# RWKV-7 rounds: K's factor, K product, seeds and K rows moved behind steps of the state chain, and one decay product for both directions

## What is computed

```
def _rwkv7_scan(r, w, k, v, kk, a, S0):
    def step(S, inp):
        rt, wt, kt, vt, kkt, at = inp
        sa = einsum('rbhvk,rbhk->rbhv', S, -kkt)
        S = S * wt[..., None, :] + sa[..., None] * (kkt * at)[..., None, :] + vt[..., None] * kt[..., None, :]
        return S, einsum('rbhvk,rbhk->rbhv', S, rt)

k_dir = k[:, :, None, :] * (1 + (a - 1) * k_a)
```

## Time and profile before

| | |
|---|---|
| time, median of 3 runs | 2148.57 us (2144.32 to 2149.24) |
| time of the profiled execution | 2146.77 us |
| span in the trace, first to last instruction | 2145.0 us (1.8 us lie around it) |
| mean granted TensorE clock | 0.940 |
| PE busy | 1885.8 us (88%) |
| DVE, ACT, POOL busy | 1031.2, 602.7, 719.9 us (48%, 28%, 34%) |
| the rounds of branch c, about 698 to 1121 us | some 423 us |

### The profile page before, as it was taken

One profiled execution on the slowest core, in us unless ns is written; L12 is line 12 of the kernel. 1 busy time (PEld: TensorE's weight loads), 2 busy tenths in 40 slices (PEclk: granted clock), 3 DMA queues, 4 the chain that ended last, 5 costly groups with the idle time before them and its releaser, 6 DMA issues. The chain is left out here.

```text
span 2145.0 us, 49387 instructions
## 1 busy us (share of the span) xinstructions
PE 1885.8 (88%) x20834; PEld 1763.5 (82%) x20834; DVE 1031.2 (48%) x1726; ACT 602.7 (28%) x1335; POOL 719.9 (34%) x560
## 2 busy tenths in 40 slices
PE   5599799998994778888773699999999999999998
PEld 3589798877992677777662599999999999999998
DVE  6703753777227454444538745434344343434254
ACT  4413244322114545455430224101111010202034
POOL 4402331442425322222302231343434353343460
PEclk8799898998998899899995699999999999999999
DMA  9554110021110000000000300111202111111122
GB/s 305 184 179 165 31 31 22 17 89 30 40 30 10 4 7 4 4 4 4 4 21 16 118 20 20 40 49 34 60 26 56 30 48 49 29 49 34 44 60 89
DMA packets 148180, 110.31 MB, mean 51 GB/s; under 512 B 13298, under 2 KB 144393, under 8 KB 147757
## 3 DMA queue, kind: packets, MB, share of 16 engines
q1 hardware_dynamic: 148013, 107.83, 16.5%
HBM read 93.17 MB, written 14.55 MB: 50 GB/s over the span
## 5 line engine op out<-in xcount | busy, mean ns | idle before, releaser
L253 PE MATMUL banks<-Z_r 128*128 128x384 f32 x2016 | 350.8, 334 | 0.0
L253 PEld LDWEIGHTS banks<-Z_r 128*128 128x128 f32 x2016 | 349.5, 188 | 0.3
L2641 DVE SCALAR_TENSOR_TENSOR XT<-banks,MOD,XT 128x128 f32 x224 | 110.7, 515 | 226.1 <-PE banks L253 225.3
L2975 ACT ACTIVATE PAD<-banks 128x384 f32<-128x384 f32 x96 | 47.2, 492 | 503.2 <-PE banks L2870 503.0
L3091 DVE TENSOR_TENSOR PAD<-PAD 128x384 f32<-128x384 f32 x96 | 99.0, 1031 | 142.9 <-ACT PAD L2975 142.8
L235 POOL TENSOR_TENSOR Z_r<-Z,ones 128x512 fp32r<-128x512 f32 x56 | 77.1, 1376 | 254.6 <-DMA Z<-in_mlp_w 254.6
L235 POOL TENSOR_TENSOR W_r<-Z,ones 128x1024 fp32r<-128x1024 f32 x32 | 77.1, 2409 | 240.4 <-DMA Z<-in_mlp_w 240.4
L2870 PE MATMUL banks<-HT_r,W_r 128*128 128x384 f32 x768 | 149.1, 335 | 2.4 <-ACT HT_r L2942 1.6
L2870 PE MATMUL banks<-YT_r,W_r 128*128 128x384 f32 x768 | 148.6, 334 | 0.0
L2870 PE MATMUL banks<-HT_r,Z_r 128*128 128x384 f32 x768 | 148.5, 334 | 0.0
L2870 PEld LDWEIGHTS banks<-HT_r,W_r 128*128 128x128 f32 x768 | 134.5, 188 | 3.3 <-issue 1.9
(11 more groups left out here) (413 smaller groups left out, 4052.7 us busy)
## 6 DMA issues: line engine op xcount, KB each, us to landing
Z<-in_w_mod SPq DMA_DIRECT2D x16, 1024.0 KB, 5.2
Z<-in_mlp_w SPq DMA_DIRECT2D x32, 512.0 KB, 4.2
Z<-in_mlp_w SPq DMA_DIRECT2D x58, 256.0 KB, 2.7
YT<-in_w_in SPq DMA_DIRECT2D x18, 512.0 KB, 3.9
XT<-in_w_mod SPq DMA_DIRECT2D x8, 1024.0 KB, 11.0
residual<-Z SPq DMA_DIRECT2D x1, 4608.0 KB, 17.5
low_part<-XT_r SPq DMA_DIRECT2D x1, 4608.0 KB, 15.6
XT<-low_part SPq DMA_DIRECT2D x8, 576.0 KB, 5.3
```

Of the source, the lines that this page charges most:

```text
L253: mm = nc.tensor.matmul(self.bank(slot, g), w[slot][:, k, :], x(k, g), start=(n == 0 and k == 0), stop=(n == 2 and k == self.blocks - 1))
L2641: ins = nc.vector.scalar_tensor_tensor(out=x, in0=S.PS[3 * slot + g][:, a:b], scalar=S.MOD[:, ds(col, 1), c:c + 1].rearrange("p a b -> p ( ...
L2975: nc.scalar.activation(R[slot][:, grp(g)], up.bank(slot, g), ACT.Relu).then_inc(up.drained[g].sem, 1)
```

## The change

Five edits, all in the rounds:

1. ACT: `q_act` and `u_act` of j = 0 stand ahead of `ka_act`.
2. DVE: the product of the state with the decay is one instruction over both directions (128x384) where it was two (128x192). For that, POOL stores the backward direction's two chunk-end decays in reversed order, so that column j is right for both directions.
3. POOL: the ones onto the diagonals come first. Then POOL waits for `new_state` of j = 0 (in rounds with a chain), makes the K product, and then the seeds.
4. DVE: the K rows come behind `zm_dve` of step 0, before `state_dve` of j = 1.
5. POOL waits for its own K product ahead of the seeds (an order that the list has anyway).

```diff
--- before.py
+++ after.py
@@ -2210,13 +2210,14 @@
 
     def round_act(act, chain, nxt, after, par):
         r, n, a = chain, nxt, after
+        if r is not None:
+            q_act(act, r, 0)
+            u_act(act, r, 0)
         if n is not None:
             tok = direction_tiles(act, n)[0]
             for d in range(2):
                 ka_act(act, n, d, tok[d])
         if r is not None:
-            q_act(act, r, 0)
-            u_act(act, r, 0)
             q_act(act, r, 1)
             u_act(act, r, 1)
         for d in range(2):
@@ -2283,10 +2284,9 @@
         heads = lambda x: x.rearrange("p d q n -> p (d q) n")
         nc.vector.tensor_tensor(heads(C.S), heads(C.S), by_block(bank(6)), ALU.add).then_inc(f["added"].sem, 1)
         done(dve, "added", r, j + 1)
-        for d in range(2):
-            ins = nc.vector.tensor_tensor(C.S[:, d, :, :], C.S[:, d, :, :],
-                                          C.ends[par][:, d, :, chunk(d, j)].unsqueeze(2).to_broadcast([P, NP, N]), ALU.mult)
-        ins.then_inc(f["new_state"].sem, 1)
+        ends = C.ends[par].rearrange("p d q j -> p (d q) j")[:, :, j]
+        nc.vector.tensor_tensor(heads(C.S), heads(C.S), ends.unsqueeze(2).to_broadcast([P, 2 * NP, N]),
+                                ALU.mult).then_inc(f["new_state"].sem, 1)
         if between:
             between()
         if j:
@@ -2332,8 +2332,6 @@
                 done(dve, "gram_l", n, d + 1)
                 nc.vector.tensor_tensor(C.LP[:, d, :, :, :].rearrange("p c q n -> p (c q) n"), by_block(bank(d)),
                                         mask(d, LEVELS, 2 * NP), ALU.mult).then_inc(f["masked_l"].sem, 1)
-            for d in range(2):
-                k_rows_dve(dve, n, d)
         if r is not None:
             state_dve(dve, r, par, 0, tiles, first if n is not None else None)
         elif n is not None:
@@ -2341,6 +2339,8 @@
         if n is not None:
             zm_dve(dve, n, 0, 0)
             zm_dve(dve, n, 0, 1)
+            for d in range(2):
+                k_rows_dve(dve, n, d)
         if r is not None:
             state_dve(dve, r, par, 1, tiles)
         if n is not None:
@@ -2378,7 +2378,8 @@
     def r_rows_pool(pool, a, d, par, tok):
         end = N if d == 0 else 0
         done(pool, "exped", a, d + 1)
-        nc.gpsimd.tensor_copy(C.ends[par][:, d, :, :], C.EP[:, d, :, :, end]).then_inc(f["ends"].sem, 1)
+        ends = C.EP[:, d, :, :, end]
+        nc.gpsimd.tensor_copy(C.ends[par][:, d, :, :], ends[:, :, ::-1] if d else ends).then_inc(f["ends"].sem, 1)
         for p in range(NP):
             ins = nc.gpsimd.tensor_tensor(tile_cols(C.RR[par][:, d, :, :], p),
                                           S.Z[:, p, ds(tok, P)].rearrange("p (c n) -> p c n", n=N),
@@ -2388,9 +2389,6 @@
     def round_pool(pool, chain, nxt, after, par):
         r, n, a = chain, nxt, after
         if n is not None:
-            tok = direction_tiles(pool, n)[0]
-            for d in range(2):
-                k_dir_pool(pool, n, d, tok[d])
             for d in range(2):
                 done(pool, "masked_l", n, d + 1)
                 nc.gpsimd.tensor_tensor(C.LP[:, d, :, :, :].rearrange("p c q n -> p (c q) n"),
@@ -2399,6 +2397,12 @@
                                             f["unit_l"].sem, 1)
             before(pool, "tz", n)
             done(pool, "unit_l", n, 2)
+            if r is not None:
+                done(pool, "new_state", r, 1)
+            tok = direction_tiles(pool, n)[0]
+            for d in range(2):
+                k_dir_pool(pool, n, d, tok[d])
+            done(pool, "k_dir", n, 2)
             for d in range(2):
                 for h in range(2):
                     x = rows_of(h)
```

## The result

| | before | after |
|---|---|---|
| median (4 runs of each, side by side) | 2146.45 us (2142.76 to 2149.24) | **2122.3 us** (2118.47 to 2127.98) |
| time of the profiled execution | 2146.77 us | 2118.47 us |
| span in the trace | 2145.0 us | 2115.5 us |
| rounds, first mask of the prologue to the last sum into Y | 411.5 us | 385.55 us |
| PE's wait for the copy of Q (list) | 12.3 us | 5.7 us |

The ratio is 0.9891, with an interval of 0.9862 to 0.9919: 23 us faster, between 17 and 30.

A forecast was written before the change was run, and what follows sets the result against it. It took the bound to be a chain passing between engines, mostly PE, with PE's idle time winnable. 6.4 + 9.1 - 2.5 - 1.0 plus 0.5 for the clock made 12.5 us: forecast 2135.0 us, range 2125 to 2144.

The forecast's parts named there:

- Part 1: ACT's factor behind the copies: PE's wait for Q falls from 1.50 to 0.58 us in seven rounds, gaining 6.4 us.
- Part 2: One state product on DVE with POOL still: PE's wait ahead of j = 1 becomes 1.33 us, gaining 9.1 us.
- Part 3: POOL's K products and seeds behind `new_state`: PE newly waits for seeds, 0.3 us over eight rounds, costing 2.5 us.
- Rival A: Each K row holds POOL's seeds up 0.56 us; eight rounds lose 0.9 us each; total gain 7 us; chance 0.17.
- Part 4: DVE's K rows behind `zm_dve`: they end at about +6 us from PE's restart, delay `tanh_act`, and cost nothing.
- The prologue: Before the chain, K products ahead of the seeds delay `tz_pe` of d = 1: costs 1 us, bounds 0 and 2.5.
- Clean rounds: Rounds at full clock take 41.3 to 41.6 us, from 43.3; over 42.3 us would mean the prediction is wrong.
- The clock: Falls to half speed behind PE's waits become fewer but are drawn anew by the spacing: 0.5 us gained.
- rival D: With shorter PE waits, clock falls become rare: 8 us more gained, 2127 us; chance 0.13.
- The stock of what could be won: Time lost to low clock in rounds 2 to 5, against the clean 43.3 us: over 10 us.
- The prediction's own test: Prediction is wrong if time lost to low clock differs from 10 us by more than 8.
- The base: Gains subtracted from the profiled execution's 2146.8 us, which stood 1.8 us under the median of 2148.6.

The follow-up runs named there:

- q_first: Kernel before with only ACT's copies of Q and U of j = 0 moved ahead of K's factor: 2145.34 us, ratio 1.0025.
- all_but_q: Changed kernel with K's factor back ahead of ACT's copies of Q and U: 2133.92 us, ratio 0.9966 to the kernel before.
- one_product: Kernel before with only the state product merged into one instruction, POOL's seeds still beside it: 2134.69 us, ratio 0.997.
- two_products: Changed kernel with the state product split into two instructions again, POOL still idle beside them: 2124.62 us, ratio 0.9935 to the kernel before.
- before_warm24: Kernel before with 24 useless matmuls in PE's wait for the state product: 2138.25 us, ratio 0.9978.
- both_warm: Kernel before with useless matmuls in both PE waits, 24 in the state product's and 12 in Q's: 2136.73 us, ratio 0.998.
- seeds_early: Changed kernel with three of POOL's four seeds ahead of its wait for `new_state`, K products last: 2122.92 us, ratio 0.9917 to the kernel before.
- before_warm: Kernel before with 48 useless matmuls in PE's wait for the state product: 2144.63 us, ratio 1.0018.
- after_hole: Changed kernel with an unused 0.96 us DVE reduction between sum and state product of j = 0: 2133.37 us, ratio 0.9957 to the kernel before.

## Why the prediction was right or wrong

**Waits against times, all kernels.** The sum of waits is what the lists show against the kernel before's 12.3 + 21.1 us; the prologue's 0.5 us is left out; the measured difference is the ratio's, at 2142 us.

| kernel | by the waits | measured (interval) | time at the lower clock, change (estimate) |
|---|---|---|---|
| q_first | +6.2 | +5.4 (+1.5 to +9.2) | +2 |
| all_but_q | -5.9 | -7.3 (-11.3 to -3.2) | -16 |
| one_product | -5.1 | -6.4 (-10.3 to -2.6) | -12 |
| two_products | -11.6 | -13.9 (-20 to -8) | -22 |
| changed kernel | -12.4 | -23 (-30 to -17), again -20 (-27 to -13) | again -34 |
| before_warm24 | 0 | -4.7 (-7.7 to -1.7) | -22 |
| both_warm | 0 | -4.3 (-7.1 to -1.3) | -29 |

The last column is an estimate of mine from all runs: every run has the mean granted clock of its whole execution on record, and twice the missing share times the span is its time at 1.2 GHz. The column is the kernel's mean less that of the kernel before beside it, in us, each good to about 10 (to 15 or so where there are only 6 or 7 runs). The 93 executions of the kernel before have a mean clock of 0.941, 253 us at the lower level; the 11 of the changed kernel have 0.948, 220 us. That is 32 us less (23 to 42). Among the 93, each us more at the lower level went with 0.28 us more of time (0.22 to 0.33), which is what the rounds gave above. So the clock's share in the lasting gain is some **9 us** (6 to 12), provided that the time at the lower level is what made those executions longer.

**Part 1: held.** 0.57 us in every round, list 12.3 to 5.7 us: 6.6 won, 6.4 forecast. But the step was costed as if it stood alone, and alone it loses 5 us (q_first). The prediction gave as cover "some 5 us ahead of the next thing that ACT owes PE"; it left out that DVE's K rows, through POOL, wait for the factor too, ahead of the state's sum. In the full change edit 4 had moved them, so no number was wrong; the parts are not to be added one by one.

**Part 2: held.** 18 products of 557 ns, none longer than 560, 0.56 forecast:

```profile
L2288 DVE TENSOR_TENSOR PAD<-PAD,misc x18: 557/557/560, 746.9 to 1090.0; 128x384 f32<-128x384 f32 x18
```

The wait is 1.34 us (1.33 forecast), the list 12.1 (12.0 forecast). Of its two causes, POOL's standing still would have done nearly all of it alone (two_products), which the prediction did not say.

**Part 3: held.** 0.29 us in a clean round where 0.3 was taken, 1.4 us in the one round that has no decay products of tile a between PE's restart and `tz_pe`; 3.2 us in the list over seven waits and 0.89 more in the prologue, where 2.5 and 1.0 were counted. Rival A, the seeds that bind, did not come. (Its own sum was loose: from +6.1 to +7.1 is 1.0 us a round and 8 us in eight, where it has 0.9 and 7.5.) With two K rows beside them the four seeds took 4.28 us, where 3.86 had been with the two products of the state and three took 2.89 in seeds_early: 0.2 us for a K row. The rule of the Trainium skill (SBUF — State Buffer, section "SBUF: two separate sides") that one engine "fully blocks" the other would have made it 0.56 for each, and the seeds 5.0; an estimate, from that rule and these rows. DVE's side fits it better, since its K rows took 1.0 us each where 0.56 is the undisturbed time. The trace agrees with a loss that lies mostly with DVE (0.9 us on the two K rows, which take 1.02 together undisturbed in seeds_early, against 0.4 on the seeds), not with a full block of GpSimd.

**Part 4: held.** The K rows took 1.95 us the pair and ended 5.7 us behind PE's restart (about 6 forecast); `tanh_act` waited 1.34 us for them, and no PE wait appeared behind it.

**The prologue** took 35.58 us against 35.05: 0.5 us, 1 forecast.

**Clean rounds** took 40.6 to 42.4 us, 41.6 on the mean, 41.3 to 41.6 forecast; the longest just passes the 42.3 us that the prediction had named as a sign of being wrong. They spread by PE's own pauses ("issue" in the list), 0.7 us each on the mean and up to 1.5, which come in some rounds and not in others; both kernels have some 10 to 14 us of them.

**The clock: this step failed.** The term of the sum that was mis-sized is the 0.5 us for the clock. The prediction read rightly that falls stand behind PE's waits and then counted 0.5 us, on the ground that "the new spacing draws it anew", with 8 us more as rival D at a chance of 0.13. The runs showed no new draw: with both waits short, none of three profiles fell at either place (17 and 3 falls in three before), and rival D is what came. In the profiled pair the clock gave some 14 us (26.0 less 11.9), lastingly some 9 by all runs and 6 by the profiles' rounds. The stock of what could be won was short too: it took four rounds (some 10 us), while all rounds of that profile stood at the lower clock for 49.2 us, 13 to 16 us at the prices above.

To lose the falls behind the waits took both waits, the one for the copy of Q and the one for the product. With only one short or filled, falls appeared at the other in three profiles (all_but_q, before_warm24, before_warm), though not in one_product. The clock's gain is not all or nothing, though: with one wait treated, the runs stood 12 to 22 us less at the lower clock (one_product, all_but_q, before_warm24, before_warm), with both treated 17 to 34 us less (seeds_early lowest). The prediction's own test, that the time lost to low clock must not differ from 10 us by more than 8, was failed in the profiled execution (0.4 us lost) and would be met by the mean of the three (some 3 us).

**The base.** The sum was made against the first profiled execution and its median, 2148.6. In four later sets of 17 to 30 runs the kernel before took 2140.2 to 2143.6 us. So the gain that lasts is 20 to 23 us. From the mean of the 93 runs, 2141.5, less 11.9 for waits and prologue and 8.9 for the clock, comes 2120.7; the 11 runs of the changed kernel have 2121.6. With 8.9 in place of 0.5 us for the clock the prediction's sum gives 2126.6, inside the range; the 4.3 us from there to 2122.3 are the base, whose median of three runs stood 5 to 8 us above the later ones. Outside the rounds the two programs are the same, and yet the stretch ahead of the rounds took 702 to 714 us from profile to profile.

**What stays open.** The clock's price is bounded, not measured: 6.2 us by three profiles each, some 9 (6 to 12) by the clock of all runs, 4.3 (1.3 to 7.1) by filling, which costs something itself. Why the changed kernel still falls 20 to 31 us into some rounds, in one profile three times and in another never, was not tried. Nor is it known what PE's "issue" pauses are.

## What to carry to other kernels

Where a trace shows clock falls behind waits (here of 1.5 to 4 us), count their removal as a gain of its own (here half to three quarters of what the waits gave). Count it in full only if all such waits of the loop go, since the clock may fall at the next one that is left; with one of two gone somewhat over half of it was seen here. Before you add up edits, ask of each what it does without the others: moving a producer back is free only for consumers that aren't ahead of something critical in their own engine's order. And take a second profile of the kernel before as base: here two executions of the same program differed by 9.5 us within the stretch in question.

## What the runs showed of the hardware

- The granted clock fell to its lower level, for 3.4 us mostly, behind PE waits of 2.65 us in five to seven of eight rounds, and behind waits of 1.50 us in five of eight once the longer one was gone (all_but_q). Behind 4.06 us it fell in eight of eight (q_first), behind 2.2 us in three (after_hole), behind 1.87 us in two (one_product, where none fell behind the 1.50 us of Q). Behind 1.34 and 0.57 us, when both were as short as that, it fell in none of three profiles, nor in two_products. A fall cost some 0.9 us of a chain in which PE is busy for four fifths.
- Matmuls of no use keep the clock up and are not free: with 12, 24 or 36 more in a round PE's unexplained pauses rose from some 10 to 14 us to 17, with 48 to 18, and with 24 in the changed kernel to 22.5.
- POOL and DVE side by side: a 128x384 product of DVE takes 0.56 us alone and 1.09 beside POOL's seeds, two of 128x192 together 0.63 alone (two_products) and 1.87 beside seeds. POOL's four seeds grew by 0.2 us for each K row and not at all for the two shorter products (3.86 us for four, where three beside nothing took 2.89). So all of the loss is DVE's beside the shorter products, and some two thirds of it beside the K rows.
